# Products of values and probabilities from 16-bit parts instead of 32-bit operands

## The reference

```python
# first block, per layer: x + ffn(x); x + mixer(x); x + ffn(x)
def one_block(args):                     # in the mixer, 8 heads, top 64 keys by an index score
    s = jnp.einsum('bqhd,bqkhd->bhqk', qb, k_sel).astype(jnp.float32) * att_scale
    s = jnp.where(valid[:, None], s, -jnp.inf)
    p = jax.nn.softmax(s, axis=-1).astype(v.dtype)
    return jnp.einsum('bhqk,bqkhd->bqhd', p, v_sel)
...
# second block, per layer: four branches of 4 heads each
y_a = flat(dilated_window_attention(...)) * jax.nn.silu(c["a_gate"])
y_b = flat(mla_attention(...)) * jax.nn.silu(c["b_gate"])
y_c = flat(nsa_attention(...)) * jax.nn.silu(c["c_gate"])      # compressed, selected and window parts
y_d = flat(stick_breaking_attention(...)) * jax.nn.silu(c["d_gate"])
for i, y in enumerate((y_a, y_b, y_c, y_d)):
    gate = jax.nn.sigmoid(h @ w_merge[l, i] + b_merge[l, i])
    merged = merged + gate * (y @ w_branch[l, i])
```

## Time and profile before

| | us |
|---|---|
| median of 3 runs | 1563.98 (1563.72 to 1564.4) |
| the profiled execution | 1563.95 |
| its span, first to last instruction | 1562.2 |
| TensorE busy | 1529.6 (98%) |
| GpSimd busy | 1015.5 (65%) |
| VectorE busy | 532.4 (34%) |
| ScalarE busy | 425.4 (27%) |

### The profile page before, as it was taken

One profiled execution on the slowest core, in us unless ns is written; L12 is line 12 of the kernel. 1 busy time (PEld: TensorE's weight loads), 2 busy tenths in 40 slices (PEclk: granted clock), 3 DMA queues, 4 the chain that ended last, 5 costly groups with the idle time before them and its releaser, 6 DMA issues.

```text
span 1562.2 us, 35975 instructions
## 1 busy us (share of the span) xinstructions
PE 1529.6 (98%) x15774; PEld 1370.2 (88%) x15774; DVE 532.4 (34%) x1311; ACT 425.4 (27%) x1120; POOL 1015.5 (65%) x550
## 2 busy tenths in 40 slices
PE   6999999999999999999999999999999999999997
PEld 5888988889888998899889988899788889878887
DVE  3111175434111221116734411115533334443333
ACT  3111163413111121105441311114532223442312
POOL 6877576666776676766666577666565565656561
PEclk9999999999999999999999999999999999999999
DMA  8656454455555565655545466545554564554451
GB/s 350 212 192 210 163 207 163 166 185 217 192 209 193 190 237 195 205 188 190 186 154 194 168 218 205 200 165 176 188 177 158 172 206 156 177 179 165 164 196 44
DMA packets 42635, 293.44 MB, mean 188 GB/s; under 512 B 4720, under 2 KB 6256, under 8 KB 8304
## 3 DMA queue, kind: packets, MB, share of 16 engines
q1 hardware_dynamic: 42480, 291.16, 53.7%
HBM read 290.09 MB, written 1.05 MB: 186 GB/s over the span
## 4 chain that ended last, share of the span: by engine, by line
PE 91%; DVE 4%; ACT 3%; issue 1%; DMA 1%; POOL 0%; SPq 0%; DVEq 0%; ACTq 0%
PE ps L548 27%; PE ps L549 27%; PE ps L550 27%; PE ps L567 1%; PE ps L569 1%; PE ps L568 1%; PE ps L667 1%; PE ps L661 1%; DVE work L1522 1%; PE ps L653 1%; DVE work L1519 1%; DMA ring<-in_w 1%; POOL w_low L524 0%; PE ps L651 0%; ACT ps L1071 0%
## 5 line engine op out<-in xcount | busy, mean ns | idle before, releaser
L524 POOL TENSOR_TENSOR w_low<-ring 128x1024 f16<-128x1024 f32 (+1 forms) x546 | 1015.3, 1884 | 513.4 <-DMA ring<-in_w 513.2
L548 PE MATMUL ps<-hP,ring 128*128 128x256 f16 (+1 forms) x3264 | 826.9, 263 | 7.3 <-POOL w_low L524 4.8
L549 PE MATMUL ps<-hP,ring 128*128 128x256 f16 (+1 forms) x3264 | 826.9, 263 | 0.0
L550 PE MATMUL ps<-hP,w_low 128*128 128x256 f16 (+1 forms) x3264 | 826.8, 263 | 0.0
L548 PEld LDWEIGHTS ps<-hP,ring 128*128 128x128 bf16 x3264 | 320.7, 98 | 47.4 <-issue 7.5
L549 PEld LDWEIGHTS ps<-hP,ring 128*128 128x128 bf16 x3264 | 320.2, 98 | 29.8
L550 PEld LDWEIGHTS ps<-hP,w_low 128*128 128x128 f16 x3264 | 320.1, 98 | 29.8
L549 PE MATMUL ps<-work,ring 128*128 128x256 f16 (+1 forms) x1328 | 312.8, 254 | 0.0
L548 PE MATMUL ps<-work,ring 128*128 128x256 f16 (+1 forms) x1328 | 312.5, 253 | 0.0
L550 PE MATMUL ps<-work,w_low 128*128 128x256 f16 (+1 forms) x1328 | 312.0, 253 | 0.0
L1402 DVE TENSOR_TENSOR ps<-work,ps 128x256 f32<-128x256 f32 x88 | 37.8, 429 | 324.5 <-PE ps L550 324.5
(11 more groups left out here) (221 smaller groups left out, 1191.4 us busy)
## 6 DMA issues: line engine op xcount, KB each, us to landing
ring<-in_w SPq DMA_DIRECT2D x264, 1024.0 KB, 4.8
ring<-in_w SPq DMA_DIRECT2D x6, 512.0 KB, 3.6
con<-in_const SPq DMA_DIRECT2D x1, 2620.0 KB, 17.8
gm<-in_gm SPq DMA_DIRECT2D x2, 1024.0 KB, 17.6
ring<-in_w SPq DMA_DIRECT2D x2, 768.0 KB, 4.2
ring<-in_w SPq DMA_DIRECT2D x2, 560.0 KB, 5.0
ring<-in_w SPq DMA_DIRECT2D x2, 544.0 KB, 3.6
xT<-in_x SPq DMA_DIRECT2D x4, 256.0 KB, 4.1
```

Source lines behind the costliest of these rows:

```text
L524: nc.gpsimd.tensor_tensor(w_low[:, c % SLOTS, a:b], ring[:, c % SLOTS, a:b], w_high[:, c % SLOTS, a:b], ALU.subtract).then_inc(split.by((c ...
L548: nc.tensor.matmul(bank, w_high[:, slot, a:a + m], rhs(k, 0), start=(k == 0), stop=False)
L549: nc.tensor.matmul(bank, w_high[:, slot, a:a + m], rhs(k, 1), start=False, stop=False)
L550: mm = nc.tensor.matmul(bank, w_low[:, slot, a:a + m], rhs(k, 0), start=False, stop=(k == kt - 1))
```

## The change

The products of values and probabilities of the twelve softmax units are made from 16-bit parts, as the products with weights are.

- ScalarE's copy writes the turned probabilities as 16 bits, into part 0 of a new view `probsTP` (heads, two parts, tokens) in the place of `probsT`.
- VectorE gets a new step `low_turned`: PSUM less part 0 gives part 1. It stands in VectorE's order behind `normalise` in A and in unit `w`, behind the two `ag` gates in unit `a`, behind the four `rope` steps in unit `s` and behind `merge(0, 3)` in unit `b`.
- GpSimd gets `split_values`: value less its own upper half gives its 16-bit low part. Each waits for the value's last `take` and stands in front of the chunk that comes three after the one that holds the value's weights.
- TensorE's `mix` waits for `turned_low` and `v_split` and runs 24 matmuls instead of 8, the two heads of a pair in turn: high by part 0, high by part 1, low by part 0.

Branch d keeps its 32-bit product. The low parts take new room in the work area.

```diff
+        def value_parts(at, n, low_at):
+            high = work[:, at:at + TT * n].bitcast(BF16).rearrange("p (t n two) -> p t n two", t=TT, two=2)[:, :, :, 1]
+            return high, work[:, low_at:low_at + n].bitcast(F16).rearrange("p (t n) -> p t n", t=TT), low_at + n
...
+VALUES = [(s, "v", "v") for s in MIX_A] + [(s, kind, piece) for s in MIX_B for kind, piece in (("av", "av"), ("cvg", "cvg"), ("bv", "mla"))]
...
             @block.gpsimd
+                def split_values(s, kind):
...
+                    pool.wait_ge(*taken(s, (kind, 3 if kind == "v" else 1)))
+                    nc.gpsimd.tensor_tensor(low, v, high, ALU.subtract).then_inc(v_split.by((s, kind)), 1)
+
                 for c in range(NCHUNK):
+                    for s, kind, piece in VALUES:
+                        if c == PLACE[s, piece, 1 if kind == "v" else 0][0][0] + 3:
+                            split_values(s, kind)
                     if SPLIT[c]:
...
-                def mix(s, u, v):
-                    pe.wait_ge(*turned_copied.at((s, u)))
-                    mix_values(v).then_inc(mixed.by((s, u)), 1)
+                def mix(s, u, v_of, high, low):
+
+                    pe.wait_ge(*v_split.at((s, v_of)))
+                    pe.wait_ge(*turned_low.at((s, u)))
+                    for h in range(0, 4, 2):
+                        for t, (out, tok) in enumerate(((slice(0, T), slice(0, T)), (slice(P, T), slice(T, PACK)))):
+                            for i, (v, part) in enumerate(((high, 0), (high, 1), (low, 0))):
+                                for g in (h, h + 1):
+                                    o = HD * (g % 2)
+                                    mm = nc.tensor.matmul(ps[o:o + HD, 4 + h // 2, out], v(t, g), probsTP[:, g, part, tok],
+                                                          start=(t == 0 and i == 0), stop=(t == 1 and i == 2))
+                    mm.then_inc(mixed.by((s, u)), 1)
...
                 def copy_turned(s, u):
                     act.wait_ge(*turned.at((s, u)))
-                    nc.scalar.activation(probsT[:, :, :], ps[:, 4:8, 0:PACK], ACT.Copy).then_inc(turned_copied.by((s, u)), 1)
+                    nc.scalar.activation(probsTP[:, :, 0, :], ps[:, 4:8, 0:PACK], ACT.Copy).then_inc(turned_copied.by((s, u)), 1)
...
+                def low_turned(s, u):
+                    dve.wait_ge(*turned_copied.at((s, u)))
+                    nc.vector.tensor_tensor(probsTP[:, :, 1, :], ps[:, 4:8, 0:PACK], probsTP[:, :, 0, :], ALU.subtract
+                                            ).then_inc(turned_low.by((s, u)), 1)
...
                     gate("ag", 0), gate("ag", 1)
+                    low_turned(s, "a")
                     dve.wait_ge(*mixed.at((s, "a")))
...
-                    merge(0, 1), merge(0, 2), merge(0, 3), merge(0, 4)
+                    merge(0, 1), merge(0, 2), merge(0, 3)
+                    low_turned(s, "b")
+                    merge(0, 4)
                     dve.wait_ge(*mixed.at((s, "b")))
```

## The result

The changed kernel takes 1574.95 us (median of 4 runs, 1573.77 to 1576.12), the kernel before 1563.85 beside it: a ratio of 1.0073, with a 95% interval of 1.0055 to 1.0090, or 11.1 us more. The forecast was 5.8 us more (1569.8), with a range of 1566.5 to 1577. The sign was right and the size about half.

What follows compares the result with a forecast made beforehand. TensorE, busy 98% of the span, was taken to bound the kernel. 1563.95 + 13.9 (stalls) - 4.2 (product) - 3.9 (GpSimd's standing still) = 1569.8 us, 0.37% more; range 1566.5 to 1577.

Steps and rivals of the forecast that it cites:

- What bounds the kernel: TensorE, busy 98% of the span: its stillness or work counts in full, other engines' work only where TensorE waits.
- Part 1, the stalls: Before the products in A and B, TensorE waits for copy and then VectorE's `low_turned` (1.76 us): +13.9 us.
- the six at 0.73: Units of A and unit w of B: product starts 0.73 us later in each of six, 4.4 us.
- Part 2, the product: Twelve products of values and probabilities: 24 paired 16-bit matmuls take 1.16 us against 1.51, -4.2 us.
- The rival that weight loads limit it: 16-bit product: loads make the 128-column slots cost 0.11 us, 1.49 us per product, nothing gained, 1574.0 us; chance 0.14.
- Part 3, GpSimd: GpSimd's eight splits and its waiting for values cause no TensorE wait for weights: 0, up to +2 us.
- Part 4, what its standing still gives: GpSimd's waiting frees VectorE's `keyset` steps and `blk` split, so TensorE waits less: -3.9 us, bounds 0 and -4.3.
- nothing to take it back: Behind each product the engines go on in the old order, so the 13.9 us of stalls stays as summed.
- The clock rival: TensorE's clock falls in the two 2.8 us stalls, costing 2.6 us each: 1575.1 us; chance 0.04.

Runs made afterwards that it cites:

- splits-only kernel: Kernel before plus GpSimd's value splits alone: 32-bit product after ScalarE's copy, no low part on VectorE; 1560.14 us, ratio 0.9980.
- the kernel with the new order and the 32-bit product: GpSimd's splits with the 32-bit product and no low part, reordered so more gemms stand between turn and product; 1559.27 us, ratio 0.9969.

## Why the prediction was right in sign and half in size

- **What bounds the kernel: right.** TensorE's own work, its waits and its clock account for the difference between the traces; GpSimd's and VectorE's added work shows only where TensorE waits for it.
- **Part 1, the stalls: right.** Forecast 13.9, measured 13.7 by the view of waits and some 14.5 from start to start. Unit by unit: 0.73 to 0.81 for the six at 0.73, 1.88 and 1.90 for the 1.81 of s, 2.69 for the 2.79 of a, 0.14 and 0.15 for the 0.14 of b. The rate (1.756 us for 1.76) and the queue of tanh, gate and low part were read off the trace of before as they came.
- **Part 2, the product: right, slightly undersized.** 1.11 us in place of 1.16, so -4.8 and not -4.2. The rival that weight loads limit it fell: its 1.49 us was not seen in any kernel at full clock. The Trainium skill ("TensorEngine Tiling (Array Packing)", "Restrictions") states that column tiling disables the fast weight load. No run here shows which kind of load an instruction used; what they show is that 24 loads of 64 columns fit beside 24 matmuls in 1.11 us, so that the loads did not set the time.
- **Part 3, GpSimd: right.** No wait for weights in A or B. GpSimd went on from 248.41 in A0, where I had 248.43 for the end of its wait.
- **Part 4, what its standing still gives: right.** -4.0 in the pair of traces, -3.8 in the splits-only kernel, -3.9 forecast. The `blk` split took 0.65 us.
- **The step that failed is a missing term.** I wrote of the stalls that I found "nothing to take it back", and left the clock to a rival with a chance of 0.04 and a price of 2.6 us for each of two stalls. It happened at four places and cost 1.3 to 1.7 us at each, 6.0 in all by the traces and 5.5 by the kernel that keeps TensorE busy. Two errors are in it. The evidence against it, waits of 1.2 us that left the clock at 1.00 (the longest inside A and B of that trace is 1.44, in B1), says nothing of stillness of twice that length; the rows said only "not seen", and 0.04 was far too sure. And I looked for such places by the length that a stall *grows* by: 2.79 for a, 1.81 for s. In unit s 0.7 us of waiting was there already, so TensorE stood still for 2.57 us, nearly as long as in a, and the clock fell there as well.
- **The price of one was too high**, 2.6 for 1.3 to 1.7 us. The windows behind a stall inside the kernel lack 1.7 us of full clock, in three of the four stalls in part while TensorE was still anyway, while the 22 us at the kernel's end, from which I took it, hold idle time of TensorE for good, and with it more time at half speed than one stall brought. The clock rival's own total, 1575.1, lies beside the measured 1574.95 by luck: half the places at nearly twice the price.

With 6.0 us for the clock the forecast's own sum gives 1575.8, and the median is 1574.95.

## What to carry to other kernels

A wait on the bounding engine has two prices: its length, and what the engine's clock does behind it; add up the whole stillness at the place, the old wait and the new, and compare it with the longest that a trace shows to have left the clock alone. Anything beyond that is unknown, not harmless. Before a product is split into cheaper parts, put enough other work between its input and the product for the step that makes the parts: here the same instructions were 11 us slower or 10 us faster than before by their order alone. And an engine that runs ahead of need can slow another one by sharing memory with it; letting it wait at the right place cost nothing and gave 4 us.

## What the runs showed of the hardware that was not expected

**Half speed after 2.6 us of stillness.** With each stall of 2.57 to 2.69 us inside B0 and B1 came a fall from 2.4 to 1.2 GHz, in six of six cases in two kernels (the changed one, and units s of the one with the low part ahead of the gate). By the trace's records of the clock it came 2.1 to 3.3 us after TensorE had stopped: in three of the six before the product began, in three within the first 0.8 us of it, which is why the price of one differs. Stalls of 0.73 to 0.81 us brought no fall, nor did the 1.24 us of the earlier trace rows, the 1.44 us at the same place in B1, or a wait of 1.59 us for `cmp_probs` in B0 of the kernel with the new order and the 32-bit product. Nothing was tried between 1.59 and 2.57.

**The start runs at half speed, and the granted clock doesn't say so.** In the first gemms of the first FFN, matmuls of 128 columns start 0.107 us apart, and then, in mid-gemm, 0.055. The changed kernel:

```profile
20.82 0.31 PE L572 MATMUL ps<-hP,ring 128*128 128x128 f16 x1
20.92 0.30 PE L573 MATMUL ps<-hP,ring 128*128 128x128 f16 x1
...
21.12 0.22 PE L572 MATMUL ps<-hP,ring 128*128 128x128 f16 x1
21.18 0.22 PE L573 MATMUL ps<-hP,ring 128*128 128x128 f16 x1
```

```profile
20.00:21.00 1.00, 1.00 (x12) 1.00 0.71 303
```

128 columns in 0.107 us are 1.2 GHz, in 0.055 nearly 2.4, yet the window of 20 to 21 us (the last row) reads 1.00. The trace's first record of the clock is at 21.09 us, the very moment at which the spacing changes; ahead of it there is none, and the column shows 1.00. The Trainium skill ("TensorE: Matmul & The Clock Gate", "The HAM clock gate (the "warmup" mystery)") says that the slow state is the default and activity releases it, and the spacing agrees. The kernel before has the same start, and its trace was open to me: TensorE's first matmul comes after 9.3 us without work, and behind it matmuls are at half speed until 24.2 us. I missed that because I read the clock's column and not the spacing. It would have told me that half speed is a state to reckon with, though not what length of a stall brings it.

**The moment at which it ends differs from run to run.** It was 21.1 us in the profiled execution of the changed kernel, 24.2 in that of before, and between 21.8 and 24.5 in the eight others, whose programs are all the same up to there. Each us later is half a us of TensorE's work. Of the 1.95 us by which the changed kernel came to A0 earlier, 0.97 were there at 14.6 us already, from shorter waits for the first weights, and the other 1.0 came between 21 and 24 us, while only the kernel before ran at half speed. The runs of one kernel spread by 1.5 to 4.4 us here; how much of that the start makes isn't shown, since only one run of each has a trace, but the ten traces differ in it by up to 3.4 us, or 1.7 us of work. So spans of single executions are compared to no better than about 2 us; the starts inside a stage are good to 0.1 us.
